# A streaming encoder step on one core: norm sums turned through rows, and VectorE's order around additions and scores

## The reference

```python
def trunk(x, ...):
    for i in range(DEPTH):                       # DEPTH = 2
        xn = rmsnorm(x, g_mix[i])
        if i % 2 == 0:                           # mLSTM: 4 heads, key width 128, value width 256
            y = mlstm_mixer(xn, state, a_w_in, a_b_gate, a_g_out, a_w_out)
        else:                                    # chunk MLP: 128-frame chunks, inner width 2048
            y, v = chunk_mlp_mixer(xn, b_w_in, b_g_v, b_w_s, b_b_s, b_w_out)
        x = x + y
        x = x + swiglu(rmsnorm(x, g_ffn[i]), f_w_gu[i], f_w_down[i])   # inner width 2816
    return rmsnorm(x, g_final)

def rmsnorm(x, g):
    return x * rsqrt(mean(x * x, axis=-1) + 1e-6) * g

def mlstm_chunk(carry, inp):                     # one head, one chunk
    s = einsum('bhtd,bhsd->bhts', q, k) * d      # scores times exp(...)
    num = einsum('bhts,bhsv->bhtv', s, v) + w_inter * einsum('bhvd,bhtd->bhtv', C, q)
    C_new = decay * C + einsum('bhs,bhsv,bhsd->bhvd', w_s, v, k)

def chunk_mlp_mixer(xn, w_in, g_v, w_s, b_s, w_out):
    u, v = split(gelu(xn @ w_in), 2)
    v = layernorm(v, g_v)
    sv = (w_s, lower triangle, per chunk) applied to v, + b_s
    return (u * sv) @ w_out, v

def swiglu(xn, w_gu, w_down):
    g, up = split(xn @ w_gu, 2)
    return (silu(g) * up) @ w_down
```

## Time and profile before

| | |
|---|---|
| median of three runs | 2811.1 us (2810.7 to 2816.9) |
| profiled execution, its own time | 2806.7 us |
| span of the trace | 2811.1 us |
| PE busy | 2772.0 us (99%) |
| DVE, ACT, POOL busy | 1538.8, 740.4, 1112.2 us (55%, 26%, 40%) |
| HBM | 49 GB/s over the span |
| chain that ended last | PE 90%, DVE 7%, ACT 1%, issue 1% |

### The profile page before, as it was taken

The page is one execution under the profiler, slowest core; times in us unless marked ns, Lnnn a source line. Parts: engine busy times, 40 slices in busy tenths (PEclk is TensorE's granted clock), DMA queues, the critical chain, the costliest instruction groups (busy, mean ns, idle before and its releaser), DMA issues.

```text
span 2811.1 us, 48611 instructions
## 1 busy us (share of the span) xinstructions
PE 2772.0 (99%) x18486; PEld 2729.3 (97%) x18486; DVE 1538.8 (55%) x2886; ACT 740.4 (26%) x1476; POOL 1112.2 (40%) x731
## 2 busy tenths in 40 slices
PE   9999999999999999999999999999999999999998
PEld 8899999999999999999899999999999999999998
DVE  4554462896555555556611465700575555555556
ACT  5202020452222222223411311300432222222224
POOL 4232323135444444444334143343244444444441
PEclk9999999999999999999999999999999999999999
DMA  3322222211111111111111111111111111111112
GB/s 106 81 78 40 69 47 64 44 38 46 45 45 45 45 45 45 45 45 52 31 46 38 54 54 38 45 45 37 40 36 46 45 45 45 45 45 45 45 45 87
DMA packets 188197, 139.19 MB, mean 50 GB/s; under 512 B 6899, under 2 KB 176715, under 8 KB 188108
## 3 DMA queue, kind: packets, MB, share of 16 engines
q1 hardware_dynamic: 188108, 137.96, 17.0%
HBM read 127.32 MB, written 10.62 MB: 49 GB/s over the span
## 4 chain that ended last, share of the span: by engine, by line
PE 90%; DVE 7%; ACT 1%; issue 1%; DMA 0%; SPq 0%; POOL 0%; ACTq 0%; DVEq 0%; POOLq 0%
PE ps L1252 32%; PE ps L901 23%; PE ps L1297 18%; PE ps L1370 7%; PE ps L1073 4%; PE ps L1430 1%; DVE xn_lo L2038 1%; DVE xs_lo L2394 1%; DVE xs_lo L2045 1%; PE ps L1476 1%; PE ps L1187 1%; PE ps L1159 1%; PE ps L1193 0%; PE ps L1189 0%; PE ps L1167 0%
## 5 line engine op out<-in xcount | busy, mean ns | idle before, releaser
L1252 PE MATMUL ps<-xs_hi,w_lo 128*128 128x288 f32 x2496 | 743.1, 298 | 0.0
L1252 PE MATMUL ps<-xs_hi,w_hi 128*128 128x288 f32 x2496 | 739.0, 296 | 3.9 <-DVE hidden L2350 2.3
L1252 PE MATMUL ps<-xs_lo,w_hi 128*128 128x288 f32 x2496 | 742.6, 297 | 0.0
L829 POOL TENSOR_TENSOR w_lo<-w_raw,w_hi 128x512 fp32r<-128x512 f32 x304 | 401.5, 1323 | 586.7 <-ACT w_hi L1671 586.1
L803 POOL TENSOR_TENSOR w_hi<-w_raw,ones 128x1024 fp32r<-128x1024 f32 x80 | 193.8, 2423 | 789.6 <-PE ps L901 559.1
L1252 PEld LDWEIGHTS ps<-xs_hi,w_hi 128*128 128x128 f32 x2496 | 470.7, 189 | 6.3 <-DVE hidden L2350 2.8
L1252 PEld LDWEIGHTS ps<-xs_lo,w_hi 128*128 128x128 f32 x2496 | 470.1, 188 | 0.3
L1252 PEld LDWEIGHTS ps<-xs_hi,w_lo 128*128 128x128 f32 x2496 | 468.9, 188 | 0.0
L1671 ACT ACTIVATE w_hi<-w_raw 128x512 fp32r<-128x512 f32 x304 | 190.0, 629 | 791.0 <-PE ps L1252 277.9
L2377 DVE TENSOR_TENSOR xT<-xT,ps 128x384 f32<-128x384 f32 x528 | 287.3, 552 | 194.4 <-PE ps L1297 186.6
L1297 PE MATMUL ps<-hg_hi,w_hi 128*128 128x384 f32 x1008 | 339.0, 336 | 3.9 <-DVE hg_lo L2369 3.2
(11 more groups left out here) (329 smaller groups left out, 4987.0 us busy)
## 6 DMA issues: line engine op xcount, KB each, us to landing
w_raw<-in_f_w_gu_dram SPq DMA_DIRECT2D x88, 512.0 KB, 3.9
w_raw<-in_f_w_down_dram SPq DMA_DIRECT2D x44, 512.0 KB, 3.3
w_raw<-in_b_w_in_dram SPq DMA_DIRECT2D x32, 512.0 KB, 4.0
w_raw<-in_a_w_in_dram SPq DMA_DIRECT2D x24, 512.0 KB, 4.6
w_raw<-in_b_w_out_dram SPq DMA_DIRECT2D x16, 512.0 KB, 3.6
out_dram<-y_out SPq DMA_DIRECT2D x9, 512.0 KB
x_in<-in_x_prompt_dram SPq DMA_DIRECT2D x8, 512.0 KB, 6.2
c_nat<-in_state_C_dram SPq DMA_DIRECT2D x8, 512.0 KB, 8.6
```

The source lines that it names most:

```text
L829: nc.gpsimd.tensor_tensor(left(layer, w_lo, pos), src, left(layer, w_hi, pos).bitcast(F32), ALU.subtract).then_inc(left_lo, 1)
L1252: ins = pe.matmul(out, left(layer, w, pos)[:, k, :], r[:, s, x, k, :], start=(first and k == 0 and m == 0), stop=(last_one and k == KH - 1 ...
```

## The change

- Heads: TensorE's heads 1 to 3 are written out in place of the loop; the other engines keep theirs. In every head DVE's `qw` comes behind the three `dmat` multiplications, and TensorE leaves out the product of the first tile with the state, which is zero there.
- FFN norms: the sums are taken by rows, in two parts (six tiles, then three), ACT takes the root of 6 and 3 elements, DVE the reciprocal of as many, spreads it on a diagonal (`f_diag`, 768 and 384 elements), TensorE multiplies ones with the diagonals, ACT copies the result to `rstd_f`. The first four gate pieces are scaled before the second part, the other four behind it.
- Chunk MLP: the 24 `lower` and the first group's sums are placed by `LOWS_WITH` and `SUMS_WITH` among the additions, with twelve `lower` behind them; `rstd_b` comes from the reciprocals that `r_tok` holds already, by one diagonal; the rows' sums go to the upper half of bank 4, and tile 8 comes last.
- Last weights: the pieces' order in `U_PIECES_LAST` changes; GpSimd splits the second unit of `W_BO` one step earlier and the third once 42 of the 48 parts of `p_lo` are written.
- End: the tables place the first group's sums, root and turns one addition later on TensorE; DVE adds that group's squares one addition earlier. The sums themselves stay on the engines where they were.

```diff
-U_PIECES_LAST = U_PIECES[:6] + [(u, g) for g in range(NG) for u in (2, 3)]
+U_PIECES_LAST = U_PIECES[:6] + [(2, 0), (2, 1), (3, 0), (3, 1), (2, 2), (3, 2)]
+LOWS_WITH = {**{m: m - 1 for m in range(1, 9)}, **{m: m - 3 for m in range(11, 15)}}
+SUMS_WITH = {15: 0, 16: 1, 17: 2}
-TURN_AFTER = {15: 0, 17: 1, 19: 2, 22: 3}
+TURN_AFTER = {16: 0, 18: 1, 20: 2, 22: 3}
-ROWS_AFTER = {13: 0, 22: 1}
+ROWS_AFTER = {14: 0, 22: 1}
...
+            split_unit(W_BO, 0, 0)
+            split_unit(W_BO, 0, 1, (used, W_BO.count(0, 1, 1 + FREE_UNITS - 3)))
+            pool.wait_ge(ps_lo, len(P_ORDER) - 6)
+            split_unit(W_BO, 0, 2)
+            split_unit(W_BO, 0, 3)
+            with pool.Fori(1, KD // 2) as i:
...
-                    pe.matmul(bank(t, DV + 1), dmat[:, c, :], v_tok[:, c, :], start=True, stop=False)
-                    if c < NP:
+                    ins = pe.matmul(bank(t, DV + 1), dmat[:, c, :], v_tok[:, c, :], start=True, stop=(c == 0))
+                    if 0 < c < NP:
...
-            head(0)
-            with pe.Fori(1, H) as h:
+            for h in range(H):
                 head(h)
...
+                def rows_first(part):
+                    b, at = F_ROWS_AT[part]
+                    for c in F_PARTS[part]:
+                        pe.wait_ge(summed, NG * (n - 1) + c // TPG + 1)
+                        c0 = at + c - F_PARTS[part][0]
+                        ins = pe.matmul(ps[b][:, c0:c0 + 1], rstd_f[:, c * P:(c + 1) * P], ones[:, 0:1],
+                                        start=True, stop=True)
+                    ins.then_inc(f_rows, 1)
+                def spread_first(part):
+                    pe.wait_ge(f_turned, 2 * layer + part + 1)
+                    for b, at, c, count in F_SPREAD[part]:
+                        pe.matmul(ps[b][:, at:at + count * P], ones[:, :], f_diag[:, c:c + count, :],
+                                  start=True, stop=True).then_inc(f_spread, 1)
...
-                    if at == 5:
-                        sum_first(0)
-                        sum_first(1)
-                    if at == 6:
-                        sum_first(2)
-                    if b > 4:
-                        pe.wait_ge(r_root, NG * (n - 1) + 8 - b)
+                    if at == 4:
+                        rows_first(0)
+                    elif at == 5:
+                        bank_free(5)
+                        spread_first(0)
+                        pe.wait_ge(f_root, 2 * layer + 1)
+                    elif at == 6:
+                        pe.wait_ge(f_norm, N_SPREAD * layer + 2)
+                    elif at == 7:
+                        rows_first(1)
                     first_piece(0, c, q)
+                spread_first(1)
...
-                    v_half(group, V_ROUNDS[1][0:2], 0)
-                    pe.wait_ge(d_add[0], N_DOWN * N_FFN + 8)
-                    row_sums(2, 7)
-                    v_half(group, V_ROUNDS[1][2:], 0)
+                    v_half(group, [5, 6], 0)
+                    row_sums()
+                    v_half(group, [7], 0)
+                    v_half(group, [5, 6, 7], 1)
+                    v_half(group, [8], 0)
+                    v_half(group, [8], 1, 8)
...
+                def inverse(part):
+                    c0, c1 = F_PARTS[part][0], F_PARTS[part][-1] + 1
+                    dve.wait_ge(f_root, 2 * layer + part + 1)
+                    dve.reciprocal(r_tok[:, c0:c1], r_tok[:, c0:c1]).then_inc(f_inverse, 1)
+                    dve.wait_ge(f_inverse, 2 * layer + part + 1)
+                    dve.tensor_tensor(f_diag[:, c0:c1, :], ident[:, :].unsqueeze(1).to_broadcast([P, c1 - c0, P]),
+                                      r_tok[:, c0:c1].unsqueeze(2).to_broadcast([P, c1 - c0, P]), ALU.mult)\
+                        .then_inc(f_turned, 1)
...
+                root(0)
+                spread(0)
                 for pos in (6, 7):
                     round_first(pos, first_mm, 16 * layer + 6)
...
+                root(1)
+                for at in range(4):
+                    gate_first(at)
+                spread(1)
                 for s in range(2):
                     act.wait_ge(x_diff, 2 * layer + s + 1)
...
+                for at in range(4, 8):
+                    gate_first(at)
+                for pos in (8, 9):
+                    round_first(pos, first_mm, 16 * layer + 8)
```

More of the change, by code:

```diff
@@ L1269, in first_piece @@
                     ins.then_inc(first_mm, 1)
-                def sum_first(g):
-                    pe.wait_ge(summed, NG * (n - 1) + g + 1)
-                    pe.matmul(bank(7 - g), ones[:, :], tok(rstd_f[:, :], g), start=True, stop=True).then_inc(r_sum, 1)
+                def rows_first(part):
[11 more added lines that the diff above has]
+                                  start=True, stop=True).then_inc(f_spread, 1)
                 def down(i, first):
@@ L2494, in body @@
                             late(m)
-                        if before_mixer and m > 0:
-                            lower(2, G_MIX + KD, *BY_GROUP[m - 1])
+                        if before_mixer and m in LOWS_WITH:
+                            lower(2, G_MIX + KD, *BY_GROUP[LOWS_WITH[m]])
+                        if before_mixer and m in SUMS_WITH:
+                            add_up(2, 0, [SUMS_WITH[m]])
                     if before_mixer:
-                        lower(2, G_MIX + KD, *BY_GROUP[-1])
+                        for n_ in range(len(LOWS_WITH), NG * KD):
+                            lower(2, G_MIX + KD, *BY_GROUP[n_])
                 with dve.Fori(0, N_FFN - 2) as i:
@@ L2504, in _ @@
             ffn(0, 1, G_FFN)
-            for g in range(NG):
+            for g in range(1, NG):
                 add_up(2, g)
```

141 lines of the change are left out of this document (79 added, 62 removed).

## The result

The changed kernel took 2795.47 us (median of 8 runs, 2792.20 to 2803.89) against 2811.05 (8 runs, 2807.31 to 2816.89): ratio 0.9945, 95% interval 0.9935 to 0.9956. The forecast was 2796.9. Its profiled execution took 2794.05 us, with a span of 2792.2.

A forecast was written before the change was run, and what follows sets the result against it. TensorE, busy 2772.0 of 2811.1 us, was taken as the bound; -4.7 + 2.1 - 1.3 - 4.5 - 4.8 - 1.0 = -14.2 gave 2796.9 us, with 2790 to 2804.5 expected 8 times in 10.

The forecast's parts named there:

- FFN norms: Start of both FFNs: reciprocals leave VectorE, but it is next late, so `down` starts 0.65 us earlier each; -1.3 us.
- Chunk MLP: Ahead of the chunk MLP: additions first, VectorE's last sum 3.0 us earlier, waits at tiles 7 and 8 gone; -4.5 us.
- Last weights: Output weights: waits of 1.45 us and 5.1 us with half clock go, +1.7 at part 45; -4.8 us.
- End: Last products: the 1.71 us wait for the sum goes, the first turn waits 0.7 for the root; -1.0 us.
- First head: First head: TensorE starts state updates 3.5 us earlier and should keep its clock, last tile at 126.4; -4.7 us.
- Heads 2 to 4: Later heads: `qw` behind `dmat` delays VectorE 1.3 us against 0.57 slack; +0.7 a head, +2.1 us.
- GpSimd holds the sixteen multiplications: FFN start: GpSimd's two 2.80 us subtractions hold VectorE's sixteen to 606.5 against 607.1; `down` gains 0.65 us, not 2.2.
- both FFNs have this shape: FFN norms: the first FFN's 0.65 us earlier `down` was taken for both FFNs, -1.3 us.
- Writing the heads out: TensorE's heads written out instead of looped: costed at nothing, as neither loop return nor written-out head showed a pause.
- VectorE keeping ahead: Rival: sums in heads 2 to 4 hide behind TensorE, FFNs win all TensorE gives; -20.7, 2790.4 us; chance 0.13.
- the pauses did not come back: Rival in which pauses come back a step later, at most places, leaving -2.6, 2808.5 us; chance 0.17.
- the clock held in heads 2 to 4: Rival denied here: new waits between tiles drop TensorE to 1.2 GHz; +6.2, 2817.3 us; chance 0.05.

The follow-up runs named there:

- the second trace of the changed kernel: The changed kernel run again as it is, on the same chip as the three gains together: 2794.75 us (6 runs), ratio 0.9937 to the kernel before.

## Why the prediction was right

Sum predicted -14.2, measured at the places -13.8; between the medians -15.6. That they agree so well is in part luck: inside two of the terms the parts miss in both directions, and the half clock, which comes and goes between executions of one program, is worth as much as a term. Term by term (after less before, from the table):

- **First head**, predicted -4.7, measured -5.1: 3.4 at the first state update (4.6 less the 1.2 us by which this execution came early to the head already), 1.7 from there to the streams' tile. The mechanism was right: the wait for `dmat` and the half clock went, and `qw` ahead brings them back.
- **Heads 2 to 4**, predicted +2.1, measured +2.16 (0.98, 0.98, 0.20). I had one wait at tile 5; in the second and the third head there are three, at one tile after another, 1.39 us in all with the slower product behind each, of which the product left out pays 0.41. The mechanism was right, VectorE's delay less the slack. That the sum fits is luck: I took the second head's slack for all three, and in the fourth the chain of states takes 4.11 us in place of 4.73 (in both kernels), so that most of the delay is hidden there.
- **FFN norms**, predicted -1.3, measured -1.1 (-1.13 and +0.07). The step that GpSimd holds the sixteen multiplications was right in size too (9.17 us, 9.2 forecast), and is shown by the run that moves it away. What failed is "both FFNs have this shape", -0.65 each: counted from the first gate product, the sixteen start 2.80 us sooner in the first FFN and only 1.61 in the second, where the first root waits for ScalarE's squares, and the same 1.67 of holding is taken from both. The sum fits by luck. What I had missed is behind them: VectorE and ScalarE take turns for the last pieces, and there 1.65 us an FFN lay.
- **Chunk MLP**, predicted -4.5, measured -3.8: 2.5 up to the first tile, 1.3 from there to the mix. Up to the last group's row sums it came as forecast: counted from the first `down` they start 2.96 us earlier (3.0 forecast), bounded by VectorE's last sum, with the first group's sums held where I had them held; the widest of them took its bare time, 1.76 us. Only TensorE's pause is divided otherwise, 1.46 us at the row sums and 1.0 at the second tile, where I had 3 at the row sums. The mis-sized step is behind them: 0.9 in place of 1.5. The waits for the root and the GELU went, but I had left the half-clock stretch as it is. It now lies over working products alone (17 in 3.4 us), before it had the second wait in it (14 products in 3.4 us): the 30 products behind the row sums take 5.15 us, 6.21 before, and 3.62 in the second trace of the changed kernel, at full clock. Another 0.2 is lost from there to the mix.
- **Last weights**, predicted -4.8, measured -4.75 (-1.57 and -3.18). Right in size, wrong in one mechanism. I had GpSimd's third split hold two `p_lo`, and TensorE wait 1.7 us at part 45 for VectorE. It is the other way round: none of the last `p_lo` was held, GpSimd's split was, and TensorE waited 2.24 us for that. (The second unit's split, a piece earlier, held four `p_lo` for 0.6 us in all, 3.5 forecast.) The 3.18 also rests on chance: the kernel before had 3.4 us at half clock here, and of the eleven later traces that wait for `w_lo` two had it too and won 1.5.
- **End**, predicted -1.0, measured -1.3 (from the first `down` to the last product). The first turn waits 0.64 us, about what I said, but behind an addition of VectorE, not the root. In four of the twelve later traces with the new tables 3.4 us at half clock fell into the end and took 1.6 us back.
- **Writing the heads out**, predicted 0, measured 0.

What the sum leaves out in the two traces, -18.4 us between the last products: -1.2 at the start and -3.2 in the rest of the output weights, both different from execution to execution with the same program. The chances: VectorE keeping ahead did not come (heads 2 to 4 grew), the pauses did not come back, and the clock held in heads 2 to 4.

The Trainium skill, SBUF — State Buffer, section SBUF: two separate sides, gives the port pair to whoever starts first, for the whole instruction. For single instructions the traces agree (`qw` 3.50 us beside a split, the sums). For rows of instructions that VectorE issues without a gap the runs show three different outcomes. The row of `p_lo` (0.55 us long, 0.47 apart), already running when GpSimd's split was let go, kept it out through 9 us. Where GpSimd had the pair as the same row began, the two took turns one by one, 2.7 us a `p_lo`. And the sixteen multiplications (0.51 us long, 0.43 apart) let GpSimd in, though they had started 0.2 us ahead of it: the second and the third took 1.56 and 1.54 us. What decides between the first and the third is not shown; operation, width and the number already issued all differ.

## What to carry to other kernels

Move an operation behind another only where something is waited for there: the same exchange won 5 us in the head where the port was taken and lost up to 1.4 in a head where it was hidden. Where two engines share a port, don't assume that letting the one go sooner makes it ready sooner: here a release 6.6 us earlier changed nothing, since the other engine's row kept the port, and giving that one instruction to a third engine won 2.3 us. When whole runs differ by 16 us by chance, cut the traces at the same products, compare the segments that the change touches, and look at the granted clock in each before you compare it.

## What the runs showed that I had not expected

**Two paces.** Over the same 100 us of the output weights, all at full clock, TensorE issued 568 products in the kernel before and 579 after: 176.7 and 173.3 ns each. Windows of the kernel before and of the changed one:

```profile
1850.00:1950.00 100.00, 100.00 (x568) 1.00 0.14 42
```

```profile
1850.00:1950.00 100.00, 100.00 (x579) 1.00 0.14 43
```

The program is the same there. Two executions of the changed kernel differ in this way over 600 us of the first FFN:

```profile
700.00:1300.00 600.00, 600.00 (x4115) 1.00 0.15 45
```

```profile
700.00:1300.00 600.00, 600.00 (x4141) 1.00 0.15 45
```

The pace holds through whole stretches: the rest of the output weights takes 164.84 or 168.01 us in all fourteen traces, nothing between, and the first FFN up to the chunk MLP (its waits taken off) 723.2 or 727.0 in thirteen of them. In the kernel before, the slower pace began as the half clock ended, at 1815.7, but half clock is not its condition: with `qw` ahead in all heads the pace went from 173.3 to 176.7 ns across TensorE's wait for `w_lo` at full clock, and in the run with the first group's sums behind it went from 176.7 to 173.3 there. Inside the output weights it changed only across such a wait. What sets it is open; no run was made for it.

**Half clock by chance.** The wait at the row sums was 1.46 to 1.48 us in these three executions (the changed kernel's second trace, its first, then the run with GpSimd's earlier subtractions moved). The 15 us around it:

```profile
1355.00:1370.00 15.00, 13.66 (x118) 13.58 (x117) 4.18 (x5) 5.28 (x11) 3.96 (x2) 1.00 0.01 1
```

```profile
1355.00:1370.00 15.00, 13.68 (x104) 13.59 (x103) 8.40 (x9) 4.44 (x9) 0.00 (x0) 0.89 0.00 1
```

```profile
1355.00:1370.00 15.00, 13.67 (x91) 13.58 (x90) 8.87 (x10) 3.97 (x8) 0.00 (x0) 0.77 0.00 0
```

No stretch at 1.2 GHz, one of 3.4 us, or one of 6.8 us; the chunk MLP up to the mix took 237.22, 238.69 and 240.23 us. Of the thirteen traces behind the kernel before, three have no such stretch there, five have 3.4 us and five 6.8 (two of the thirteen, one without and one with 6.8, have another order of VectorE ahead of it). A pause of this length costs 0, 1.5 or 3.0 us more than itself, and one trace doesn't tell which.
